# Two decoder layers written out instead of looped, with filler products ahead of the first norm and the copies of h ahead of weight copies

## The reference, cut to what matters

```
for l in range(2):
    h = rmsnorm(x, norm1_g[l])                  # first norm
    x = x + mixing_block(h, ...)                # h @ w_in, h @ w_gate, four branches, w_branch, w_o
    h = rmsnorm(x, norm2_g[l])                  # second norm
    x = x + hier_moe(h, ...)                    # router: a group, then 2 of its 4 experts; silu(gate)*up, down
```

## Time and profile before

| | us |
|---|---|
| median of 3 runs | 861.31 (859.49 to 861.57) |
| profiled execution, its own time | 859.19 |
| its span, first to last instruction | 857.4 |
| mean granted TensorE clock | 0.966 |
| PE busy | 794.9 |
| DVE busy | 658.7 |
| ACT busy | 520.6 |

### The profile page before, as it was taken

The page is one execution under the profiler, slowest core; times in us unless marked ns, Lnnn a source line. Parts: engine busy times, 40 slices in busy tenths (PEclk is TensorE's granted clock), DMA queues, the critical chain, the costliest instruction groups (busy, mean ns, idle before and its releaser), DMA issues.

```text
span 857.4 us, 14225 instructions
## 1 busy us (share of the span) xinstructions
PE 794.9 (93%) x4794; PEld 702.9 (82%) x4794; DVE 658.7 (77%) x857; ACT 520.6 (61%) x582; POOL 15.5 (2%) x34
## 2 busy tenths in 40 slices
PE   4999999997769999999799999999777999999996
PEld 4999999996648878777699999999655887787875
DVE  7548897289376888988664799539757788889998
ACT  6435655563347788787542655476253877877776
POOL 2010000000000000000001000000000000000000
PEclk9999999999869999999799999999987999999999
DMA  7865253563323999999635635345521599999996
GB/s 230 295 198 199 98 196 99 172 221 127 119 99 120 331 343 350 348 344 344 208 117 182 244 96 176 123 149 197 195 94 56 193 333 346 336 362 339 359 343 214
DMA packets 84082, 190.71 MB, mean 222 GB/s; under 512 B 14937, under 2 KB 27700, under 8 KB 84020
## 3 DMA queue, kind: packets, MB, share of 16 engines
q1 hardware_dynamic: 84020, 189.94, 63.6%
HBM read 188.86 MB, written 1.05 MB: 221 GB/s over the span
## 4 chain that ended last, share of the span: by engine, by line
issue 89%; PE 7%; DMA 1%; POOL 1%; ACT 1%; DVE 1%; SPq 0%; DVEq 0%; POOLq 0%
PE bank L1206 2%; PE bank L1208 2%; PE bank L1207 2%; DMA raw<-in_w_in 1%; PE bank L1227 1%; ACT w_hi L475 1%; POOL qkrs L447 1%; SPq L354 0%; DVE qkss L832 0%; DVE p_t L831 0%; POOL rs L453 0%; POOL rstd L447 0%; SPq L289 0%; PE bank L1238 0%; DVE rdiag L787 0%
## 5 line engine op out<-in xcount | busy, mean ns | idle before, releaser
L724 DVE TENSOR_TENSOR w_lo<-raw,w_hi 128x2048 fp32r<-128x2048 f32 (+1 forms) x183 | 403.1, 2216 | 115.4 <-ACT w_hi L475 114.1
L475 ACT ACTIVATE w_hi<-raw 128x2048 fp32r<-128x2048 f32 (+1 forms) x183 | 338.5, 1857 | 192.7 <-PE bank L1208 145.7
L1206 PE MATMUL bank<-a_hi,w_hi 128*128 128x256 f32 x704 | 201.3, 286 | 1.6 <-DVE a_lo L797 1.6
L1207 PE MATMUL bank<-a_hi,w_lo 128*128 128x256 f32 x704 | 199.6, 284 | 0.0
L1208 PE MATMUL bank<-a_lo,w_hi 128*128 128x256 f32 x704 | 199.5, 283 | 0.0
L1206 PE MATMUL bank<-w_hi,y_lo 128*128 128x512 f32 x432 | 171.2, 396 | 0.8 <-DVE y_lo L1149 0.8
L1208 PE MATMUL bank<-w_lo,y_lo 128*128 128x512 f32 x432 | 168.6, 390 | 0.0
L1206 PEld LDWEIGHTS bank<-a_hi,w_hi 128*128 128x128 f32 x704 | 135.5, 192 | 2.7 <-DVE a_lo L797 1.8
L1207 PEld LDWEIGHTS bank<-a_hi,w_lo 128*128 128x128 f32 x704 | 135.6, 193 | 0.2
L1208 PEld LDWEIGHTS bank<-a_lo,w_hi 128*128 128x128 f32 x704 | 135.5, 192 | 0.0
L1207 PE MATMUL bank<-w_hi,y_hi 128*128 128x512 f32 x288 | 112.2, 390 | 0.0
(11 more groups left out here) (283 smaller groups left out, 891.2 us busy)
## 6 DMA issues: line engine op xcount, KB each, us to landing
raw<-in_w_e_gate SPq DMA_DIRECT2D x72, 512.0 KB, 4.4
raw<-in_w_e_up SPq DMA_DIRECT2D x72, 512.0 KB, 5.8
raw<-in_w_e_down SPq DMA_DIRECT2D x72, 512.0 KB, 5.0
raw<-in_w_gate SPq DMA_DIRECT2D x56, 512.0 KB, 4.4
raw<-in_w_in SPq DMA_DIRECT2D x38, 512.0 KB, 6.2
raw<-in_w_branch SPq DMA_DIRECT2D x16, 512.0 KB, 4.0
raw<-in_w_o SPq DMA_DIRECT2D x16, 512.0 KB, 4.0
raw<-in_w_gate SPq DMA_DIRECT2D x16, 256.0 KB, 2.7
```

The lines of the kernel that those rows point to most:

```text
L475: a.activation(w_hi[:, at.slot(n, PART), 0:w], raw[:, slot, 0:w], ACT.Copy).then_inc(hi_done, 1)
L724: v.tensor_tensor(w_lo[:, part, 0:w], raw[:, slot, 0:w], w_hi[:, part, 0:w].bitcast(F32), ALU.subtract).then_inc(split_done, 1)
L1206: mm(ps, a2[0], b2[0], start=first, stop=False, skip_group_check=shared)
L1207: mm(ps, a2[1], b2[0], start=False, stop=False, skip_group_check=shared)
```

## The change

The layers are written out in Python on all five engines; the loop over passes stays. The first three units of the kernel are no longer all split ahead of h: only a0 is, a1 and a2 come behind the copies of h on ACT and DVE. On DVE `lo` of unit 2 is moved: it was at the end of each pass and, for the first pass, ahead of the router's L1034; now it is at the top of each pass, and for the mixing block behind h_lo. `hi` of unit 2 stays where it was. PE gets `keep_warm`: 9 products of 128x256 without use ahead of the first norm of layer 0, and 7 ahead of that of layer 1, in bank 4. It waits for 8 of POOL's constants at the start, not 18. What the last layer prepared for a third (parameters, squares, `rstd_rows`) is gone, except for the loads of three weight units and their `hi`.

```diff
@@ sync
-            with sp.Fori(0, DEPTH) as l:
-                before = sp.value_load(tab[0:1, 0, 7:8], min_val=0, max_val=DEPTH * (NG + 1))
+            for l in range(DEPTH):
+                before = sp.value_load(tab[0:1, 0, 7:8], min_val=0, max_val=DEPTH * (NG + 1)) if l else 0
...
-                sp.wait_ge(S("x_mid"), 4 * (l + 1))
-                norm_gains(nxt)
-                mixer_parameters(nxt)
-                sp.wait_ge(S("gp_hi"), 2 * (before + l) + 2)
-                router_parameters(nxt)
+                if l < DEPTH - 1:
+                    sp.wait_ge(S("x_mid"), 4 * (l + 1))
+                    norm_gains(nxt)
+                    mixer_parameters(nxt)
+                    sp.wait_ge(S("gp_hi"), 2 * (before + l) + 2)
+                    router_parameters(nxt)
@@ scalar
-            for n in range(AHEAD):
-                hi(At(0, 0, False), n)
+            hi(At(0, 0, False), 0)
...
-                for n in range(AHEAD, 6):
+                for n in range(AHEAD if l else 1, 6):
                     hi(at, n)
...
-                for i in range(4):
+                for i in range(4 if l < DEPTH - 1 else 0):
                     act.wait_ge(S("x_out"), 2 * T * l + i + 1)
                     square(i // 2, i % 2)
@@ vector
-            for n in range(AHEAD):
-                lo(At(0, 0, False), n)
-            with dve.Fori(0, DEPTH) as l:
+            lo(At(0, 0, False), 0)
+            for l in range(DEPTH):
...
-                lo(at, 3)
-                lo(at, 4)
-                lo(at, 5)
+                for n in range(2 if l else 1, 6):
+                    lo(at, n)
...
                     v.tensor_tensor(xt_lo[:, t, :, :], xn[:, t, :, :], xt_hi[:, t, :, :].bitcast(F32),
                                     ALU.subtract).then_inc(S("xt_lo_done"), 1)
-                lo(at, 2)
                 dve.wait_ge(S("lt_done"), l + 1)
...
+                    lo(at, 2)
                     lo(at, 3)
                     hidden(0)
...
                     last.then_inc(S("selt_done"), 1)
-                    lo(ahead, 2)
...
-                rstd_rows(l + 1)
+                if l < DEPTH - 1:
+                    rstd_rows(l + 1)
@@ tensor
+            def keep_warm(b, n):
+                for _ in range(n):
+                    mm(bank[b][:, 0:256], ones[:, :], amask[:, :], start=True, stop=True)
+
             H = [h_hi, h_lo]
-            pe.wait_ge(pool_consts, 18)
+            pe.wait_ge(pool_consts, 8)
...
-            with pe.Fori(0, DEPTH) as l:
+            for l in range(DEPTH):
                 xk = x[:, :, :].rearrange("q t (p c) -> q t c p", c=KT)
+                keep_warm(4, 7 if l else 9)
                 for t in range(T):
```

More of the change, by code:

```diff
@@ L392, in _ @@
                 sp.dma_start(out[0, P * t:P * t + P, :], x[:, t, :]).then_inc(stored, 16)
-            sp.wait_ge(par_a, 16 * 13 * (DEPTH + 1))
-            sp.wait_ge(par_g, 16 * (DEPTH + 1))
-            sp.wait_ge(par_r, 16 * 5 * (DEPTH + 1))
+            sp.wait_ge(par_a, 16 * 13 * DEPTH)
+            sp.wait_ge(par_g, 16 * DEPTH)
+            sp.wait_ge(par_r, 16 * 5 * DEPTH)
             sp.wait_ge(stored, 16 * T)
@@ L455, in _ @@
             power1(0)
-            with pool.Fori(0, DEPTH) as l:
+            for l in range(DEPTH):
                 power("v_ms", v_rs[:, :], v_ss[:, :], T, "v_rs_done", l)
@@ L459, in _ @@
                 power("n2_ms", rstd[:, :], ssq[:, :], T, "n2_rs", l)
-                power1(l + 1)
+                if l < DEPTH - 1:
+                    power1(l + 1)
             pool.drain()
@@ L499, in _ @@
                     square(t, h)
-            for n in range(AHEAD):
-                hi(At(0, 0, False), n)
+            hi(At(0, 0, False), 0)
             act.wait_ge(S("tab_zero"), 1)
-            with act.Fori(0, DEPTH) as l:
+            for l in range(DEPTH):
                 act.wait_ge(par_g, 16 * (l + 1))
@@ L510, in _ @@
                                  scale=g1[:, k:k + 1]).then_inc(S("h_hi_done"), 1)
-                before = act.value_load(tab[0:1, 0, 7:8], min_val=0, max_val=DEPTH * (NG + 1))
+                before = act.value_load(tab[0:1, 0, 7:8], min_val=0, max_val=DEPTH * (NG + 1)) if l else 0
                 at = At(l, before, False)
-                for n in range(AHEAD, 6):
+                for n in range(AHEAD if l else 1, 6):
                     hi(at, n)
@@ L799, in _ @@
                                            op0=ALU.mult, op1=ALU.subtract).then_inc(S("h_lo_done"), 1)
-                before = dve.value_load(tab[0:1, 0, 7:8], min_val=0, max_val=DEPTH * (NG + 1))
+                before = dve.value_load(tab[0:1, 0, 7:8], min_val=0, max_val=DEPTH * (NG + 1)) if l else 0
                 step.at(n_first + DVE_STEPS * l)
                 at = At(l, before, False)
-                lo(at, 3)
-                lo(at, 4)
-                lo(at, 5)
+                for n in range(2 if l else 1, 6):
+                    lo(at, n)
                 dve.wait_ge(S("sgw_tp"), l + 1)
@@ L1230, in _ @@
                             last.then_inc(S("n1_t"), 1)
-                before = pe.value_load(tab[0:1, 0, 7:8], min_val=0, max_val=DEPTH * (NG + 1))
+                before = pe.value_load(tab[0:1, 0, 7:8], min_val=0, max_val=DEPTH * (NG + 1)) if l else 0
                 at = At(l, before, False)
```

## The result

The changed kernel takes 870.10 us (median of 8 runs, 864.82 to 873.70) against 861.25 us for the kernel before (8 runs, 858.41 to 865.42): ratio 1.0094, 95% interval 1.0064 to 1.0124. It is slower by 0.9%. I had forecast 857.8 and given slower a chance of 0.09.

What follows compares the result with a forecast made beforehand. PE, busy 794.9 of 857.4 us, was taken as the bound. Terms -2.7 + 0.1 + 0.7 - 0.9 - 2.4 + 1.7 = -3.5 took the median 861.31 to 857.8 us, range 855.0 to 861.2.

Steps and rivals of the forecast that it cites:

- tops of the other passes: Passes after each layer's first: m2's split behind three table reads would start by 302.9 and cost 0.
- rival on the other side: Tops of passes: reads not hidden, +1.1 a pass, +7.7 over 7 passes, 865.5 us; chance 0.10.
- First pass: First pass of each layer: m2's split behind four table reads makes PE wait, +0.85, twice +1.7; no wait for m6.
- Start: Kernel start: h before a1 and a2 lets PE begin a1 at 24.9, -2.7; fillers mostly hidden, +0.1.
- Norm's products: Products of the first norm: fillers' full clock would not shorten them, 0.245 against 0.24 us each; no gain.
- Turn: Layer 0 to layer 1: fillers in PE's stream end at 417.95 against 417.27, +0.7, bounds -0.6 to +2.4.
- Router: Behind the logits: L1034 no longer waits for m2's split, -1.2 a layer, -2.4 for two.
- End: Kernel end: additions to x no longer wait behind a2's split, -0.9.

Runs made afterwards that it cites:

- e2: Kernel before, loops kept, only unit 2's low-part split moved to the head of the pass (first units: behind h's low part): 872.73 us, ratio 1.0115.
- e10: Kernel before, loops kept, with only nine filler products added ahead of each layer's first norm products: 863.03 us, ratio 1.0013.
- e8: Changed kernel with hidden(1) moved ahead of m8's high copy on ACT: 864.88 us, ratio 1.0034.
- e17: Changed kernel with both transfers of m9 cut from 512 to 64 KB in layer 1's passes only: 867.75 us, ratio 1.0077.
- e1: Changed kernel with unit 2's low-part split back at its three old places: 860.83 us, ratio 0.9969.
- e7: Changed kernel without fillers, m2's split back at the pass end, for a layer's first pass behind the clearing, ahead of the reads: 857.80 us, ratio 0.9963.
- e15: Changed kernel with the second transfers of m4 and m5 cut from 512 to 64 KB: 831.27 us, but another amount of work.
- e9: Kernel before with three more table reads between `z_lo` and m2's split at each pass end: 863.17 us, ratio 1.0012.
- e12: Kernel before with one constant read into a register on SP between the two transfers of m6's load: 864.25 us, ratio 1.0034.
- e13: Kernel before with three constant reads into a register on SP between the two transfers of m6's load: 868.25 us, ratio 1.0085.
- e3: Changed kernel without its 9 and 7 filler products: 868.45 us, ratio 1.0068.

## Why the prediction was wrong

- **The step that failed: tops of the other passes.** I wrote that "m2's split may begin 0.5 + 0.4 later, up to 302.9, at no cost". The delay was sized well: the split begins 0.9 behind `z_lo` (0.13 before), the transpose's wait is gone, and PE waits only up to 0.34 for m2. What I left out is the second thing that this split does: it frees the raw buffer. I followed it for the first pass only ("no wait, with little to spare") and there I asked only when PE wants m6. I should have asked what is queued behind it: m8's transfer, on ACT `hidden(1)` behind m8's copy, and PE's m7 behind that. Price: 8.3 us at m7 in nine passes, by e2 +9.9 us (1.15% of 861) for the moved line with its gains in the router included.
- **The rival on the other side had the wrong place.** It priced reads that aren't hidden, and decided from a split later than 303.4. The split was at 303.04, under that bound, and the kernel was slower all the same.
- **First pass.** PE waited for m2 by 0.58 and 0.32, and the step to m2 grew by 0.75 and 0.48, where I had +0.85. But m6's load, leaving at 268.23 instead of 244.40, came with waits of 1.08 and 1.30 at m7.
- **Start: right.** First w_in product at 18.35 (18.37 forecast), a1 at 24.74 (24.9), against 27.58. Of these 2.84, 1.70 were gone again by the logits of layer 0, most of it where the clock fell at 100.81 (below). The fillers ended at 10.33, inside the bounds of 7.6 and 11.5.
- **Norm's products: right, and shown.** 7.64 us from the first product to the first on w_in at clock 1.00, as in layer 1 before at 0.50 for the most part (7.65); e10 is unchanged in time. The rule of N over 2.4 GHz in the Trainium skill's page "TensorE: Matmul & The Clock Gate", section "Wait — 56ns, not 53.3ns?", which has 53.3 ns for N = 128, doesn't hold for them (0.24 us). That the step of 8 floats is the reason was only argued. The trace of before bears it out: products of the same shape and type, with a stationary operand without a step, do follow the clock. Their records start 0.109 us apart at 1.00 (the first line) and 0.213 at 0.50 (the second). No run varied the step.

```profile
126.95 1.04 PE L1374 MATMUL bank<-ident,xn 128*128 128x128 f32 x8
...
234.52 3.67 PE L1457 MATMUL bank<-ident,xn 128*128 128x128 f32 x16 [5.15 <-ACT xn L486]
```

- **Turn: right in number, in part by luck.** From the first product of the last scatter to the norm's first product 6.62 us, 5.90 before (417.27 - 411.37): +0.7, the forecast's number. No idle time ahead of L1231. But the number depends on where the clock falls. Here it stood at 0.50 from 414.83 to 418.25; in e8's and e17's traces, with the same fillers, it stayed at 1.00 and the turn took 4.97 and 5.00.
- **Router: half right.** PE's wait ahead of the bias's transposes fell from 1.80 to 0.56 in both layers, the 1.2 forecast. Up to the first unit of the passes 0.8 was left in layer 0, and layer 1 lost 0.5; there the clock stood at 0.50 over the logits, which had 1.00 before.
- **End:** the part behind the last pass became 0.55 shorter, 0.9 forecast.

Without the failed step the sum agrees with the runs, within wide intervals. e1 keeps the start (-2.7 + 0.1) and the turn (+0.7), -1.9 in all, and gave -0.31%, 2.7 us. e7 keeps the start and the routers, -5.1, and gave -0.37%, 3.2 us (1.2 to 5.3). In both the last split of a pass stands ahead of the additions to x again, so the -0.9 of the end does not count. That e7's 857.80 is also the number that I had forecast is luck: it has other terms.

## What to carry to other kernels

An operation that frees a buffer has two deadlines: its own result's, and that of the load that waits for the buffer. Before moving it, follow the load to its landing, to the copy that waits for it, and to whatever stands behind that copy in its engine's stream. Here a late issue cost time at a DMA share of 0.98 over a pass and, in e15, at 0.89 too; so an average share under 1 is no proof of slack, only the row of the waiting copy is. Put reads of registers behind the operation that releases a buffer, as e7 does, not ahead of it.

## What the runs showed that I had not expected

- A load that leaves 1.05 us late made the second load behind it land 2.4 us late, with a queue that was busy for 0.52 and 0.38 of the two microseconds around its issue (0.06 and 0.05 in e15). Transfers cut ahead of it, beside it or behind it did not take the waits away.
- Reads of a table into registers are hidden at the end of a loop's body (three of them: 0.2 us on the split behind them in e9) and, behind the loop's jump, delay it by 0.75 at its head (0.88 against 0.13). On SP one took 0.56 us ((2.12 - 1.00) / 2 from e12 and e13). The Trainium skill's page "DMA: Bandwidth & Descriptors", section "🔬 Latency and other measured facts", has a floor of about 600 ns for such a load (`tensor_load`); SP's reads come out a little under it.
- The granted clock fell in the middle of a stretch in which PE had hardly rested. PE was busy for 9.94 of the 10 us ahead, at the full clock, and then, in the changed kernel:

```profile
100.81:104.22 3.41, 3.41 (x17) 3.41 (x18) 3.34 (x5) 2.80 (x13) 0.00 (x0) 0.50 0.00 0
```

The unit there took 7.35 us instead of 5.85. In the profile of before the same products ran at 1.00; in e3's and e7's the clock fell near the same place (100.22 and 101.04).
